# Rotary exchange by transfers, output pieces at the memory units, the gated heads' sums in another order, and decay tables made in the first feed-forward

## What is computed

```python
def partial_rotary(t, positions):           # heads of 64 features, the first 16 are turned
    half = ROPE_DIM // 2                    # 8
    inv_freq = ROPE_THETA ** (-2.0 * jnp.arange(half, dtype=jnp.float32) / ROPE_DIM)
    ang = positions.astype(jnp.float32)[..., None] * inv_freq
    cos, sin = jnp.cos(ang)[:, :, None, :], jnp.sin(ang)[:, :, None, :]
    t1, t2 = tr[..., :half], tr[..., half:]
    rot = jnp.concatenate([t1 * cos - t2 * sin, t2 * cos + t1 * sin], axis=-1)
...
    for l in range(DEPTH):                  # first model: l = 0 windowed attention, l = 1 RG-LRU
        h = rms_norm(x, mix_norm[l])
        kv = mem_n @ w_mem_kv[l]            # mem_n: the normed memory, 256 rows
        ...                                 # mixed, mq: the mixer's result and the memory's queries
        mo = memory_attention(mq, mk, mv)
        x = x + jnp.concatenate([mixed, mo], axis=-1) @ w_out[l]
        x = x + squared_relu_mlp(rms_norm(x, mlp_norm[l]), w_up[l], w_down[l])
```

## Time and profile before

| | us |
|---|---|
| median of 3 runs | 3268.87 (3266.75 to 3268.92) |
| the profiled execution | 3271.29 |
| its span, first to last instruction | 3269.5 |
| PE busy in the span | 3214.9 (98%), 15214 matmul records |
| DVE busy | 1791.1 (55%) |
| ACT busy, POOL busy | 1139.9 (35%), 418.0 (13%) |
| DMA engines, mean share busy | 26%, 90 GB/s |

### The profile page before, as it was taken

The page is one execution under the profiler, slowest core; times in us unless marked ns, Lnnn a source line. Parts: engine busy times, 40 slices in busy tenths (PEclk is TensorE's granted clock), DMA queues, the critical chain, the costliest instruction groups (busy, mean ns, idle before and its releaser), DMA issues. The chain is left out here.

```text
span 3269.5 us, 40332 instructions
## 1 busy us (share of the span) xinstructions
PE 3214.9 (98%) x15214; PEld 2628.6 (80%) x15214; DVE 1791.1 (55%) x1928; ACT 1139.9 (35%) x1315; POOL 418.0 (13%) x319
## 2 busy tenths in 40 slices
PE   8999999999899999999999999999999999999998
PEld 6887888877788888888877888888888877888887
DVE  7775534459754354544576664345444576664344
ACT  4453222249432222322343433223322343533221
POOL 1001000110100016000243120003000144130002
PEclk9999999999999999999999999999999999999999
DMA  4112322232122223322221122324222221122322
GB/s 151 65 59 68 106 92 101 90 110 84 52 98 95 99 94 103 119 93 103 90 73 57 52 101 83 112 81 122 107 90 103 81 86 52 65 90 83 109 86 81
DMA packets 46195, 293.17 MB, mean 90 GB/s; under 512 B 5424, under 2 KB 5936, under 8 KB 17936
## 3 DMA queue, kind: packets, MB, share of 16 engines
q1 hardware_dynamic: 44640, 287.04, 25.2%
q0 software_dynamic: 1456, 4.79, 0.9%
HBM read 289.70 MB, written 2.10 MB: 89 GB/s over the span
## 5 line engine op out<-in xcount | busy, mean ns | idle before, releaser
L1848 DVE TENSOR_TENSOR w_lo<-w_raw,w_hi 128x2048 fp32r<-128x2048 f32 (+1 forms) x285 | 664.8, 2333 | 243.8 <-ACT w_hi L1421 243.6
L885 PE MATMUL ps<-xg_hi,w_hi 128*128 128x512 f32 x1920 | 750.3, 391 | 2.2 <-DVE w_lo L1848 2.2
L885 PE MATMUL ps<-xg_hi,w_lo 128*128 128x512 f32 x1920 | 747.7, 389 | 0.0
L885 PE MATMUL ps<-xg_lo,w_hi 128*128 128x512 f32 x1920 | 747.6, 389 | 0.0
L1421 ACT ACTIVATE w_hi<-w_raw 128x2048 fp32r<-128x2048 f32 (+1 forms) x287 | 542.7, 1891 | 537.4 <-PE ps L885 357.5
L885 PE MATMUL ps<-hid_hi,w_hi 128*128 128x512 f32 x1216 | 473.7, 390 | 0.1
L885 PE MATMUL ps<-hid_lo,w_hi 128*128 128x512 f32 x1216 | 473.5, 389 | 0.0
L885 PE MATMUL ps<-hid_hi,w_lo 128*128 128x512 f32 x1216 | 473.4, 389 | 0.0
L885 PEld LDWEIGHTS ps<-xg_hi,w_hi 128*128 128x128 f32 x1920 | 360.5, 188 | 79.5 <-issue 4.8
L885 PEld LDWEIGHTS ps<-xg_lo,w_hi 128*128 128x128 f32 x1920 | 360.5, 188 | 75.7 <-issue 1.4
L885 PEld LDWEIGHTS ps<-xg_hi,w_lo 128*128 128x128 f32 x1920 | 360.5, 188 | 75.0
(11 more groups left out here) (357 smaller groups left out, 4004.7 us busy)
## 6 DMA issues: line engine op xcount, KB each, us to landing
w_raw<-up_dram SPq DMA_DIRECT2D x120, 1024.0 KB, 4.8
w_raw<-in_dram SPq DMA_DIRECT2D x42, 1024.0 KB, 4.8
w_raw<-down_dram SPq DMA_DIRECT2D x32, 1024.0 KB, 4.8
w_raw<-down_dram SPq DMA_DIRECT2D x32, 768.0 KB, 4.3
w_raw<-down_dram SPq DMA_DIRECT2D x32, 640.0 KB, 3.8
w_raw<-out_dram SPq DMA_DIRECT2D x14, 1024.0 KB, 4.9
w_raw<-out_dram SPq DMA_DIRECT2D x8, 768.0 KB, 4.3
w_raw<-memk_dram SPq DMA_DIRECT2D x4, 1024.0 KB, 4.8
```

Of the source, the lines that this page charges most:

```text
L885: last = pe.matmul(to, (w_hi, w_lo)[wp][:, q, t:t + P], parts[xp], start=(k == 0 and m == 0), stop=(k == p.ktiles - 1 and m == 2))
L1848: dve.tensor_tensor(w_lo[:, q, 0:w], w_raw[:, q, 0:w], w_hi[:, q, 0:w].bitcast(F32), ALU.subtract)\
```

## The change

Six edits:

1. **Rotary exchange.** `swaps` and the load of `rope_swap` are gone. POOL issues for each pair of tiles four transfers from `proj` to `rope_r` (8 partitions by 4 KB each: lanes 0 to 7 and 8 to 15 of both heads change places), once both tiles are read out of PSUM; `rope` multiplies `rope_r` instead of PSUM. The sign goes into `inv_freq`, so into the sine.
2. **Memory squares.** POOL's first square waits for slab 0 to be read (`evac`) instead of the token sum.
3. **Memory units of layer 0.** `weigh` stands ahead of the piece at n = 17; the pieces at 18 and 19 stand ahead of `turn_out`; the last piece (1, 4, 8) is cut in two around the last `turn_out`. The split of `out1_0`'s third slab is made in two halves.
4. **Memory units of layer 1.** Pieces of 6 matmuls at n = 1 to 6 and two behind the loop; DVE does `front(M1[1])` and the low part ahead of a split, and the next split one unit later and ahead of `back`.
5. **Gated heads.** `block(2)` goes ahead of `levels(1)`, on PE and on DVE.
6. **Decay tables.** `lam_tables` goes from behind slab 5 of the first projection to the start of `up1_0_1`, the first feed-forward's second half.

```diff
-        sp.dma_start(rope_swap[:], a["rope_swap"]).then_inc(win_in, 16)
...
-        pool.wait_ge(ss_mm, 1)
+        pool.wait_ge(evac, EV0 + Q)
         pool.wait_ge(mem_in, 16)
         pool.tensor_tensor(mem_sq[:], mem_raw[:], mem_raw[:], ALU.mult).then_inc(mem_add, 1)
...
+        def rope_halves(n):
+            if n == 0:
+                pool.wait_ge(rope_sc, 1)
+            else:
+                pool.wait_ge(rope_t, 2 * n)
+            pool.wait_ge(evac, EV0 + Q * (n + 2))
+            t0 = ROPE_TILES[2 * n]
+            for lane in (0, WIN_D):
+                for to, src in ((lane, lane + 8), (lane + 8, lane)):
+                    pool.dma_start(rope_r[to:to + 8, :, :], proj[src:src + 8, t0:t0 + 2, :]).then_inc(rope_in, 16)
+
+        for n in range(len(ROPE_TILES) // 2):
+            rope_halves(n)
...
+                if n in OUT_FILL and n + 2 >= len(us):
+                    first_out(*OUT_FILL[n])
                 if n and us[n - 1].last:
                     turn_out(us[n - 1])
...
+                weigh(u)
+                if n in OUT_FILL and n + 2 < len(us):
                     first_out(*OUT_FILL[n])
-                weigh(u)
-            if us is SECTIONS["window"]:
-                first_out(1, 4, 8)
+            first_out(1, 4, 6)
             turn_out(us[-1])
+            first_out(1, 6, 8)
...
             block(1)
+            block(2)
             levels(1)
             levels(2)
-            block(2)
...
-            def swaps(j):
...
-                    pe.matmul(ps[:, 4 + n % 2, :], rope_swap[:], proj[:, ROPE_TILES[n], :], start=True, stop=True)\
-                        .then_inc(rope_mm, 1)
...
+            def out_half(n):
+                out(0, 1, n // 2, n % 2 * 2, n % 2 * 2 + 2)
...
-                if 1 <= n < 4:
-                    out(0, 1, n - 1)
+                if 1 <= n < 7:
+                    out_half(n - 1)
                 weigh(u)
-            out(0, 1, 3)
+            out_half(6)
             turn_out(M1[-1])
+            out_half(7)
...
-                        split_high(s0 + 2, 0, p.tiles * P)
...
+                        for n, done in enumerate((out_hi, hi_done)):
+                            h = slice(6 * P * n, 6 * P * (n + 1))
+                            act.activation(w_hi[:, 0, h], w_raw[:, 0, h], ACT.Copy).then_inc(done, 1)
...
-            if slab == 5:
-                lam_tables()
...
-            dve.wait_ge(rope_mm, n + 1)
-            dve.tensor_tensor(tmp[:, n % 2, :], ps[:, 4 + n % 2, :], rope_sin[:], ALU.mult).then_inc(rope_t, 1)
+            dve.wait_ge(rope_in, 64 * (n // 2 + 1))
+            dve.tensor_tensor(tmp[:, n % 2, :], rope_r[:, n % 2, :], rope_sin[:], ALU.mult).then_inc(rope_t, 1)
...
+            front(M1[1], 1)
+            low(DT - 1)
             split(MIX_O + 1)
-            low(DT - 1)
-            front(M1[1], 1)
...
+                if n == 2:
+                    split(MIX_O + 2)
                 back(u)
-                if n == 1:
-                    split(MIX_O + 2)
...
+                if j == 1:
+                    block(2)
                 place(j)
-                if 2 <= j < NPROD - 1:
+                if 3 <= j < NPROD - 1:
                     block(j)
...
+            if p.name == "up1_0_1":
+                lam_tables()
```

More of the change, by code:

```diff
@@ L314, in program @@
     mem_in = sem("mem_in")
+    out_hi = sem("out_hi")
     win_in = sem("win_in")
@@ L368, in program @@
     rope_sc = sem("rope_sc")
-    rope_mm = sem("rope_mm")
+    rope_in = sem("rope_in")
     rope_t = sem("rope_t")
@@ L1237, in values @@
                     last.then_inc(vt_psum, 1)
-            def swaps(j):
-                if j == 2:
-                    pe.wait_ge(win_in, 48)
-                    pe.wait_ge(vt_ready, 2)
-                pe.wait_ge(evac, EV0 + Q * j)
-                for n in (2 * (j - 2), 2 * (j - 2) + 1):
-                    if n >= 2:
-                        pe.wait_ge(rope_t, n - 1)
-                    pe.matmul(ps[:, 4 + n % 2, :], rope_swap[:], proj[:, ROPE_TILES[n], :], start=True, stop=True)\
-                        .then_inc(rope_mm, 1)
             for j in range(p.slabs):
@@ L1274, in first_projection @@
                             values()
-                        elif 2 <= j < p.slabs - 1:
-                            if j == 3:
-                                memory_sums()
-                            swaps(j)
-                        elif j:
+                        elif j == 3:
+                            memory_sums()
+                        elif j == p.slabs - 1:
+                            pe.wait_ge(vt_ready, 2)
                             pe.wait_ge(rope_done, 10)
@@ L1316, in gates, with out @@
                 last.then_inc(g_mm, 1)
-            def out(h, part, b):
+            def out(h, part, b, k0=0, k1=4):
                 s = MIX_O + 3 * h + part
-                if b == 0:
+                if b == 0 and k0 == 0:
                     pe.wait_ge(lo_done, s + 1)
@@ L1324, in out @@
                     pe.wait_ge(ot_ready, M1[-1].f + 1)
-                for k in range(4):
+                for k in range(k0, k1):
                     if part < 2 and not (h or b):
@@ L1333, in out @@
                                          start=(part == 0 and k == 0 and m == 0), stop=(part == 2 and k == 3 and m == 2))
-                last.then_inc(mm_done, 1)
+                if k1 == 4:
+                    last.then_inc(mm_done, 1)
+            def out_half(n):
+                out(0, 1, n // 2, n % 2 * 2, n % 2 * 2 + 2)
             dense(0, lambda: token_rms(gained(MIX_NORM)))
@@ L1937, in resid @@
                 if p.name == "out1_0" and isinstance(i, int) and i == q == 0:
-                    split_low(s0 + 2, 0, p.tiles * P)
+                    dve.wait_ge(out_hi, 1)
+                    dve.tensor_tensor(w_lo[:, 0, 0:6 * P], w_raw[:, 0, 0:6 * P], w_hi[:, 0, 0:6 * P].bitcast(F32),
+                                      ALU.subtract)
+                    dve.wait_ge(hi_done, s0 + 3)
+                    dve.tensor_tensor(w_lo[:, 0, 6 * P:12 * P], w_raw[:, 0, 6 * P:12 * P],
+                                      w_hi[:, 0, 6 * P:12 * P].bitcast(F32), ALU.subtract).then_inc(lo_done, 1)
                 if not p.last or p.next_norm == NORMS - 1:
@@ L2468, in gated @@
                     factors(made)
+                if j == 1:
+                    block(2)
                 place(j)
-                if 2 <= j < NPROD - 1:
+                if 3 <= j < NPROD - 1:
                     block(j)
-                    if j % 2 == 0:
-                        split(3 + j // 2)
+                if 2 <= j < NPROD - 1 and j % 2 == 0:
+                    split(3 + j // 2)
             block(10)
@@ L2672, in layout @@
     lane = np.arange(P) % WIN_D
-    put("inv_freq", np.where(lane < 16, freq[lane % 8], 0).astype(np.float32)[:, None])
+    put("inv_freq", np.where(lane < 8, -freq[lane % 8], np.where(lane < 16, freq[lane % 8], 0)).astype(np.float32)[:, None])
     a["vecs"] = cols
@@ L2678, in layout @@
     a["win_mask"] = np.where(np.abs(k - P - q) <= 128, 0, NEG).astype(np.float32)
-    swap = np.zeros((P, P), np.float32)
-    for lane in range(P):
-        if lane % WIN_D < 8:
-            swap[lane + 8, lane] = -1
-            swap[lane, lane + 8] = 1
-    a["rope_swap"] = swap
     masks = np.full((P, 3, SLAB_C), NEG, np.float32)
```

8 lines of the change are left out of this document (4 added, 4 removed).

## The result

The changed kernel takes **3251.3 us** (median of 4 runs, 3248.9 to 3252.5) against 3268.9 for the kernel before (4 runs beside them): a ratio of 0.9945, with a 95% interval from 0.9933 to 0.9957. It is faster by 17.6 us. I had said 3240 with a range up to 3250, so the sign was right and the size was not.

The account below looks back on a forecast made before the run. PE was taken as the bound, busy 3214.9 of 3269.5 us. Terms 5.9 - 3.2 + 8.3 - 0.5 + 4.8 + 5.5 + 8.0 = 28.8 us saved gave 3242.5 for a profiled execution, median 3240, range 3232 to 3250.

Parts of the forecast that it names:

- squares' move: First projection: POOL's square no longer holds DVE, so PE's 3.40 us wait at the transposes shrinks and clock returns; +5.9 us.
- squares' new place: First projection: POOL's squares alternate with DVE's angle steps, so PE waits for slab 3's split; cost 3.2 us.
- swaps gone: First projection: PE no longer does the rotary swap matmuls, 1.72 us a pair for five pairs; +8.3 us.
- transfers: First projection: POOL's rotary transfers are just hidden before PE asks for unit 0's scores; cost 0.5 us, bounds 0 and 2.
- memory units, layer 0: Reordered pieces cover DVE's work at the last units and the halved split starts earlier; +4.8 us, bounds 3 and 5.5.
- memory units, layer 1: New order of pieces and splits cuts PE's 8.6 us of waits to 5.1; +5.5 us, bounds 3.5 and 7.
- gated layers: block(2) ahead of levels(1) removes PE's waits of 2.52 and 1.40; 4.0 us a layer, +8.0 for two.
- profiled execution to median: Whole kernel: the profiled execution lies 2.4 us above the median 3268.9, so the forecast median goes to 3240.
- first rival: First projection: POOL's squares don't hold DVE, the 3.2 us isn't paid; time 3234, 16 in 100.
- L: First projection: time from DVE's reading of a slab to the landing of its rotary transfers; 4.4 to 5.7, taken as 5.0 us.
- second rival: First projection, late landings: transfers land after 7.6 us, longer than PE can wait; saving 20, time 3249, 16 in 100.
- the slower case: First projection: landings of 14.2 us in all five rounds make the kernel slower, time 3282; 2 in 100.

Follow-up runs that it names:

- e2: Changed kernel with POOL's memory squares behind the first exchange's transfers and the memory's sums, gains and low parts one slab later; 3244.1 us, ratio 0.9926.
- e5: Changed kernel with SP's 1 MB loads of slabs 5 to 9 held back until the exchange's transfers before them have landed; 3244.7 us, ratio 0.9927.
- e8: Changed kernel with half of POOL's decay-difference instructions in the gated layers left out from step 3 on; 3248.1 us, ratio 0.9933.
- e13: Kernel before, unchanged, traced a second time in one execution; 3267.9 us.
- e14: Kernel before, unchanged, traced a third time in one execution; 3268.0 us.
- e15: Changed kernel with the decay tables' 24 DVE instructions behind slab 5 of the first projection again; 3251.7 us, ratio 0.9942.
- e9: Kernel before with POOL's squares waiting for ACT's root of the token sums instead of the sums themselves; 3266.5 us in 11 runs, ratio 0.9993.
- e6: Changed kernel with the exchange split by tile and the squares behind the first tiles' transfers, memory sums one slab later; 3245.2 us, ratio 0.9926.
- e3: Changed kernel with each slab's exchange split by tile, four 16 KB transfers for each tile, two semaphores; 3243.2 us, ratio 0.9923.
- e12: Changed kernel with the rotary exchange on PE again, two matmuls with rope_swap per slab; 3259.1 us, ratio 0.9966.
- e1: Changed kernel with POOL's memory squares behind the sum of squares again, ahead of DVE's first reading; 3247.4 us, ratio 0.9931.
- e10: Changed kernel with the squares waiting for ACT's root of the token sums instead of the reading of slab 0; 3247.9 us, ratio 0.9934.

## Why the prediction missed

Term by term, against the profiled executions:

| term | forecast | measured |
|---|---|---|
| squares' move | +5.9 | +5.7 |
| squares' new place | -3.2 | -2.2 |
| swaps gone | +8.3 | +8.8 |
| transfers | -0.5 | -8.3 |
| memory units, layer 0 | +4.8 | +4.5 |
| memory units, layer 1 | +5.5 | +6.3 |
| gated layers | +8.0 | +5.0 |
| sum | 28.8 | 19.8 |
| profiled execution to median | -2.4 | -0.2 |

*Squares.* Forecast by the right mechanism and, at slab 3, near the right size: in the trace POOL's square starts at 32.46, DVE's next step takes 4.09, and slab 3 waits 1.82 for its split where I had 2.4. That and the lower clock, which did not follow, are the 1.0 us of difference. The first rival, squares for nothing, is out. The 2.2 is only what the new place costs at slab 3. It also starts DVE's chain later: with the squares behind the first exchange (e2) the kernel is 7.2 us faster.

*Swaps.* Five pairs gave 1.69 to 1.77 us each, 8.8 in all; right.

*Transfers: the step that failed.* "4.4 to 5.7 us, I take 5.0 for L" gave 8.2, 6.4, 6.6 and 6.6. The formula around it was right. With the measured landings in the place of L, the chain I wrote down ends at 102.2 + 3.2 + 1.4 + 0.9 + 1.6 = 109.3, less 0.9 for its earlier start, and the trace has the last reading end at 108.1. The 5.0 itself is near what the transfers take with no load issued beside them, 4.5 to 5.5 in e5. What I left out is SP's 1 MB load, which is set off by the split right behind the same reading; holding it back (e5) takes the time to 3244.7. For the second landing, 6.4, the load is not shown to be the cause. I named it in the second rival ("SP's 1 MB loads run at the same time") and gave it 16 in 100, though rows 8 offered no small transfer without company. The lesson of the sum's shape is that it was steep: the rounds need 10.9 us at PE and took 9.65 by my L; with an L of 6.4 they take 11.05, and DVE never catches up. The 8.3 us are 1.4 at slab 4, 1.5 at slab 6, 0.4 between them and slab 7 and 5.0 before unit 0, the last with 1.6 of low clock. The statement that the splits come 1 to 5 us before PE needs them fell with it.

*Second rival.* Late landings were to give 3249, by L = 7.6. The place, the mechanism and nearly the time were this rival's (e5 shows it). That the time came so near is in part luck: the landings were shorter than its 7.6 in three exchanges of five, and 5 us were lost elsewhere, in the gated layers and at the median. Its weight was too small. What I said there of DVE's instructions is not so either: a reciprocal of DVE (75.44) starts beside POOL's last issue of the third exchange; that transfer landed in 2.1 us.

*Memory units.* By place they came 0.3 us below and 0.8 above their terms, both inside their bounds. One item inside was wrong. The halved split was to give 0.5 of the 1.01 at the third slab of `out1_0`, and the wait is 1.08. PE, POOL and DVE there:

```profile
283.76 0.49 PE L899 MATMUL ps<-mixA_hi,w_hi 128*128 128x512 f32 x1 [1.08 <-DVE w_lo L1955]
```

```profile
280.90 1.03 POOL L701 TENSOR_TENSOR ssq<-x 128x512 f32<-128x512 f32 x1 [181.41 <-DVE x L1948]
```

```profile
280.93 1.82 DVE L1952 TENSOR_TENSOR w_lo<-w_raw,w_hi 128x768 fp32r<-128x768 f32 x1 [0.18 <-ACT w_hi L1448]
282.68 0.94 DVE L1955 TENSOR_TENSOR w_lo<-w_raw,w_hi 128x768 fp32r<-128x768 f32 x1
```

Against PE the first half starts 0.7 earlier than the whole did, and so right behind POOL's sum, which holds it for 0.9: 1.82 instead of 0.94. This was read from the trace and not tried by an experiment.

*Gated layers.* I forecast the waits that go, 4.0 a layer, and they went: in the first, 18.8 us stood won behind `levels(3)`, 4.0 over the 14.8 ahead (in the second 3.3, with a new wait of 0.4 for a split). Then PE lost 0.7 at `levels(4)` and 0.5 at `levels(6)`. "No wait, or some tenths" looked at DVE's copies alone. The step I left out is POOL: with the sums earlier against the blocks, its differences run without a pause and hold DVE's splits and factors by 0.6 to 0.8 us each (e8). I knew the rule and had used it for the squares.

*Profiled execution and median.* I took the whole saving off a profiled execution that lay 2.4 above the median and moved the result down by the same 2.4. That is right only if both kinds of execution win the same. They don't: the 3.40 and its clock, 5 us of the sum, are in the profiled execution and not in two others (e13, e14). The changed kernel's profile lies at its median. This step cost 2.2 us; with 6.5 from the first projection, 3.0 from the gated layers and 0.5 given back by the units, that makes the 11.2.

*Decay tables.* 0 forecast, and by e15 at most about 1 us as long as the landings are late. They had the room I said.

*Sums of the rivals.* Two figures are off by less than 1 us: 28.8 + 3.2 saved gives 3236.9 and not 3236, and the slower case is reached at L = 12.9, not 13.5. Neither moves a chance.

Open is what makes the times of one kernel spread by 4 to 5 us where the squares can't collide (e9). Stretches at a granted clock of 0.50 that come and go between executions account for 1.7 us (e14 against before, near 162; e6 against e3) and 3 us (e12), and e13 loses 0.9 us against before in each gated layer; what sets the stretches off I did not find.

## What to carry to other kernels

Before a small transfer is put on a chain, look at what else the same event sets off: a load of 1 MB that starts with it belongs in its landing time. Where a chain's round is close to the period of the engine that waits for it, give both sides of that point their full weight: here landings 1.4 to 3.2 us longer than forecast turned a cost of 0.5 into 8.3. And before a wait of the profile is booked as a gain, look whether the profiled execution is one like the median: where two engines start within 10 ns of each other, another execution may have them in the other order.

## What the runs showed of the hardware

- DVE and POOL held each other up in these traces by who started first, and both ways: POOL's square took 3.60 us when it was not held and 5.58 when DVE's split had started 0.17 us ahead of it, while that split kept its 2.28; the next DVE step then took 4.09. The Trainium skill (SBUF — State Buffer, Who interferes with whom) says that the order of issue decides who blocks; these rows agree.
- DVE's reciprocal of 128x512 (3.35 us in e13, beside a square of 3.60 on POOL) and its readings from PSUM (1.29 for two) were not held.
- Four 32 KB transfers inside SBUF took 4.5 to 5.5 us from the reading to the landing without a load issued beside them (e5) and 4.3 to 8.2 with one (changed kernel, e1, e10). It was above all the last of the four that was late: 2.1 to 2.3 us from issue to landing where nothing delayed it, 4.2 to 5.6 where something did. ACT needed 0.63 us to issue one, POOL 0.52.
- The granted clock fell to 0.50, the 1.2 GHz level, in stretches with no new wait ahead of them, in some executions and not in others: near 162 us in e14 and not in the trace of before, which is the same code. The same holds behind a wait: after 1.82 us at slab 3 it stayed at 1.00 in the changed kernel, and after 1.85 at the same place in e3 it was 0.58 from 52 to 56.
